# A two-block transformer kernel on one core: the first block's x turned and projected tile by tile, half of a modulation chunk computed later, x turned ahead of the weight splits, the last output tile in halves

## Chip, cores and metric

One core of a Trainium2 chip runs the whole program. The metric is the device time of one execution in microseconds (us), lower is better. The profile names the engines PE (TensorE), PEld (its weight loads), DVE (VectorE), ACT (ScalarE), POOL (GpSimd) and SP (SyncE, which here only issues transfers).

## What is computed

256 tokens with 1024 features go through two blocks of two layers each, all in float32. The first block, for each layer `l`:

```
h = x @ w_in[l]                      # 1024 x 5024: latents, two gates, q, k, v, 2048 merge gates
# latent attention (8 heads) from rms-normed latents, differential attention (4 heads)
merged = sigmoid(gates)[:, :1024] * (y_a @ w_branch_a[l]) + sigmoid(gates)[:, 1024:] * (y_b @ w_branch_b[l])
x = layer_norm(DEEPNORM_ALPHA * x + merged @ w_out[l])
```

The second block modulates with vectors made from a condition `c`, and a second stream `ctx` has its own condition:

```
mod_lat = silu(c) @ mod_w[i] + mod_b[i]          # 9 vectors of 1024 a layer, 1024 x 9216 weights
mod_ctx = silu(c_ctx) @ mod_w[0] + mod_b[0]
x = half_ffn(x); ctx = half_ffn(ctx)             # h = x * (1 + scale) + shift; swiglu, 1024 -> 2816 -> 1024
x = window attention over x and ctx (layer 0) or Fourier mixing (layer 1); x = half_ffn(x)
```

The output is x, 256 x 1024 float32.

## The kernel before

**Products in three parts.** A float32 product is made of three matmuls in a rounded format (`product`, L598 to L600): high part of x by high part of w, high x by low w, low x by high w. Weights come in 1 MB transfers into five slots of `raw`, two "pieces" of 128 x 1024 in each. For every piece ACT writes the high part (`w_hi`, L1173, six places), then DVE the low part (`w_lo`, L1545, ten places). `split()` on either engine is one piece. PE takes a piece with `piece()` and frees it with `piece_done`; 490 pieces go through in all. A piece of 512 columns is 12 matmuls.

**x turned.** Before a projection PE transposes x (two tiles, `t`, of 128 tokens) into PSUM banks `turn0`, `turn1`, `score0`, `score1`; ACT writes `xT_hi`, DVE `xT_lo`. In the first block and ahead of the first FFN, `turn` goes over both tiles and `project` starts once both are there. Elsewhere in the second block `turn_tile` and `project_first` (PE) with `second_tile` (ACT, DVE) turn and project tile 0 while tile 1 is still being normed. `keep_busy` issues matmuls whose result nobody reads.

**Modulation vectors.** DVE multiplies `mod_w` rows by silu(c), feature group by feature group (`mod_feature`, L1666: once into `acc_ctx` for the ctx condition, once into `mod_run` for c). POOL loads the weights, two feature groups to a 512 KB transfer (L492), into a ring of two places: a transfer is issued when DVE has used up the one two before. Eight groups, f0 to f7, make a chunk of 512 columns; then PE sums it over partitions with 16 small matmuls (`mod_sum`, L727), and DVE stores the result (`mod_store`). Each layer of the first block does six chunks, five of them for both conditions; the fifth of these (chunk 4) is done during the last projection and the layer norm. On POOL the first chunk of a layer waits for x of both tiles, and between its fourth transfer and the next chunk's first stand `b_merge` (two of 1 MB) and the `ln_rows` (two of 512 KB).

**Order.** All engines run lists written out by hand, with semaphores; what stands ahead on an engine's list delays what stands behind. `layer_norm` on DVE (L1635 to L1646) and `norm_root` on ACT (L1237, L1239) share the norm, tile after tile.

## Time and profile before

| | |
|---|---|
| time, median of 3 runs | 1633.92 us (1633.36 to 1637.47) |
| the profiled execution: its time, its span | 1632.27 us, 1630.5 us |
| PE busy | 1568.3 us, 96% of the span |
| DVE, ACT, POOL busy | 1204.2, 795.6, 156.2 us |
| transfers | 349.61 MB, 214 GB/s on average |
| granted PE clock, mean | 0.989 |

Busy time of PE is the sum over its matmuls as far as they don't overlap, those of `keep_busy` among them; its idle time is the rest, 62 us. A row of the timeline gives start, length, engine, line, operation, tensors, shape, how many instructions are merged in it, and in brackets how long the engine sat idle before it and what ended that.

### The profile page before, as it was taken

The page shows a single profiled execution, that of the slowest core. Times are in us where ns is not written, and L with a number is a line of the kernel's source. Part 1 is how long each engine was busy: PE and PEld are TensorE (multiplying, and loading weights), DVE is VectorE, ACT ScalarE, POOL GpSimd, SP SyncE. Part 2 cuts the span into 40 slices and gives each one's busy share as a digit, 9 for nine tenths or more (in the row PEclk, how much of TensorE's full clock was granted, in tenths as well). Part 3 has the DMA queues.
Part 4 walks back from the last instruction along what each step waited for, and adds up shares of the span by engine and source line. Part 5 has one row for each costly group of instructions (what it writes and reads, how often), then busy time and mean ns, then how long its engine had stood idle before and what let it go on. Part 6 is the DMA issues. An engine that isn't in the chain of part 4 may idle for free.

```text
span 1630.5 us, 20592 instructions
## 1 busy us (share of the span) xinstructions
PE 1568.3 (96%) x7685; PEld 1297.5 (80%) x7685; DVE 1204.2 (74%) x1852; ACT 795.6 (49%) x1243; POOL 156.2 (10%) x212
## 2 busy tenths in 40 slices
PE   6999989999999999999999899999999999999997
PEld 6888868888778887788877558888888888788886
DVE  6888888888877775777858867877587775575554
...
GB/s 282 306 225 166 157 158 301 245 184 142 172 220 264 285 271 234 194 277 277 271 167 196 123 1 232 281 277 278 209 235 279 282 274 181 91 210 190 181 182 77
DMA packets 200508, 349.61 MB, mean 214 GB/s; under 512 B 11189, under 2 KB 128237, under 8 KB 199901
## 3 DMA queue, kind: packets, MB, share of 16 engines
...
HBM read 347.21 MB, written 1.08 MB: 214 GB/s over the span
## 4 chain that ended last, share of the span: by engine, by line
PE 85%; DVE 10%; ACT 1%; DMA 1%; issue 1%; SPq 0%; DVEq 0%; POOLq 0%; ACTq 0%
PE acc L598 25%; PE acc L600 25%; PE acc L599 25%; DVE w_lo L1545 2%; PE turn L962 1%; PE acc L868 1%; PE score L848 1%; PE score L1058 1%; DVE acc_ctx L1666 1%; DVE x L1646 1%; DVE att_work L2126 1%; PE turn L857 1%; DMA raw<-in_w_in 1%; DMA mod_raw<-in_mod_w 1%; DVE wide L1879 1%
## 5 line engine op out<-in xcount | busy, mean ns | idle before, releaser
L1545 DVE TENSOR_TENSOR w_lo<-raw,w_hi 128x1024 fp32r<-128x1024 f32 (+2 forms) x490 | 584.3, 1200 | 258.5 <-ACT w_hi L1173 257.7
L1173 ACT ACTIVATE w_hi<-raw 128x1024 fp32r<-128x1024 f32 (+2 forms) x490 | 503.1, 1039 | 475.5 <-PE acc L600 439.3
L598 PE MATMUL acc<-w_hi,xT_hi 128*128 128x512 f32 (+1 forms) x1440 | 572.2, 397 | 10.2 <-issue 4.8
L600 PE MATMUL acc<-w_hi,xT_lo 128*128 128x512 f32 (+1 forms) x1440 | 562.1, 390 | 0.0
L599 PE MATMUL acc<-w_lo,xT_hi 128*128 128x512 f32 (+1 forms) x1440 | 561.4, 390 | 0.0
L598 PEld LDWEIGHTS acc<-w_hi,xT_hi 128*128 128x128 f32 x1440 | 271.8, 189 | 65.1 <-issue 12.0
L600 PEld LDWEIGHTS acc<-w_hi,xT_lo 128*128 128x128 f32 x1440 | 271.6, 189 | 57.0
L599 PEld LDWEIGHTS acc<-w_lo,xT_hi 128*128 128x128 f32 x1440 | 272.1, 189 | 52.8
L492 POOL DMA_DIRECT2D mod_raw<-in_mod_w x144 | 104.1, 723 | 924.0 <-DVE mod_run L1666 741.6
L598 PE MATMUL acc<-w_hi,hT_hi 128*128 128x512 f32 x440 | 172.8, 393 | 0.0
L600 PE MATMUL acc<-w_hi,hT_lo 128*128 128x512 f32 x440 | 171.4, 390 | 0.0
L599 PE MATMUL acc<-w_lo,hT_hi 128*128 128x512 f32 x440 | 171.3, 389 | 0.0
L1666 DVE SCALAR_TENSOR_TENSOR mod_run<-mod_raw,silu_c,mod_run 128x512 f32<-128x512 f32 x216 | 160.9, 745 | 5.1 <-DMA mod_raw<-in_mod_w 5.0
L598 PEld LDWEIGHTS acc<-w_hi,hT_hi 128*128 128x128 f32 x440 | 82.6, 188 | 18.3 <-issue 1.7
L600 PEld LDWEIGHTS acc<-w_hi,hT_lo 128*128 128x128 f32 x440 | 82.6, 188 | 17.4
L599 PEld LDWEIGHTS acc<-w_lo,hT_hi 128*128 128x128 f32 x440 | 82.7, 188 | 16.8
L1404 ACT ACTIVATE silu_g<-acc 128x256 f32<-128x256 f32 x110 | 36.3, 382 | 83.0 <-PE acc L600 83.0
L1237 ACT ACTIVATE turned<-x,neg_mean 128x1024 bf16<-128x1024 f32 x16 | 18.5, 1156 | 84.3 <-DVE neg_mean L1635 84.3
L1666 DVE SCALAR_TENSOR_TENSOR acc_ctx<-mod_raw,silu_c,acc_ctx 128x512 f32<-128x512 f32 x70 | 52.1, 744 | 6.0 <-DMA mod_raw<-in_mod_w 6.0
L2027 DVE TENSOR_TENSOR hidden<-acc,silu_g 128x256 f32<-128x256 f32 x110 | 41.5, 419 | 11.9 <-ACT silu_g L1404 8.2
L1313 ACT ACTIVATE work<-score,neg_max 128x256 f32<-128x256 f32 x64 | 29.6, 472 | 31.3 <-DVE neg_max L1785 31.3
L2034 DVE TENSOR_TENSOR hT_lo<-turn,hT_hi 128x512 fp32r<-128x512 f32 x55 | 38.0, 691 | 5.7 <-ACT hT_hi L1408 5.1
...
## 6 DMA issues: line engine op xcount, KB each, us to landing
...
```

The source lines that it names most:

```text
L492: pool.dma_start(mod_raw[:, s, :, :], w_mod[l, :, 2 * i:2 * i + 2, at]).then_inc(mod_in[s], 16)
L598: nc.tensor.matmul(dst, xh, wh, start=start, stop=False)
L599: nc.tensor.matmul(dst, xh, wl, start=False, stop=False)
L600: return nc.tensor.matmul(dst, xl, wh, start=False, stop=stop)
L1173: nc.scalar.activation(piece_part(w_hi[:, i % SPLIT_SLOTS, :], i), piece_part(raw[:, s, i % 2 * PIECE:(i % 2 + 1) * PIECE], i), ACT.Copy). ...
L1237: step(nc.scalar.activation(squares[:, t, :], x[:, t, :], ACT.Square, bias=neg_mean[:, t:t + 1], accum_out=square_sum[:, t:t + 1]))
L1313: m = nc.scalar.activation(p[:, t * TOK:t * TOK + TOK], bank[b][:, t * TOK:t * TOK + TOK], ACT.Exp, bias=neg_max[:, h, 2 * m_ + t:2 * m_ + ...
L1404: nc.scalar.activation(silu_g[:, half, t, :], bank[ACC[2 * half + t]][:, FC:2 * FC], ACT.Silu).then_inc(silu_done, 1)
L1545: nc.vector.tensor_tensor(piece_part(w_lo[:, i % RAW_PIECES, :], i), piece_part(raw[:, i // 2 % RAW_SLOTS, i % 2 * PIECE:(i % 2 + 1) * PIE ...
L1666: m = nc.vector.scalar_tensor_tensor(out=end if k == KD - 1 else run, in0=w, scalar=by, in1=run, op0=ALU.mult, op1=ALU.add)
L2027: nc.vector.tensor_tensor(hidden[:, half, t, :], bank[b][:, 0:FC], silu_g[:, half, t, :], ALU.mult).then_inc(moved[b], 1)
L2034: nc.vector.tensor_tensor(sl(hT_lo), bank[b][:], sl(hT_hi).bitcast(F32), ALU.subtract).then_inc(moved[b], 1)
```

## The change

1. *Start.* ACT no longer makes silu(c) and the exponential of lambda (each with a table load) ahead of the first splits; it does two splits instead of five before it writes `xT_hi`, and DVE likewise two instead of three. PE does 2 `keep_busy` matmuls instead of 6 and 5.
2. *Arrival of weights.* Each half of a slot has a semaphore of its own, and ACT's split of a piece waits for its half alone (except where halves are columns: the FFN's up weights).
3. *Tile by tile.* Layer 1's first projection and the first FFN's go through `project_first`. At the end of layer 0 the engines turn tile 0 with `plain_tile(0)` during tile 1's norm, at the end of layer 1 with `turn_tile`, as the second block does.
4. *Half of a chunk put off.* f4 to f7 of chunk 4 (and its `mod_sum`, now after the second projection) move from the end of a layer into the next layer's first splits, or the first FFN's (`owed`).
5. *Branches.* Feature groups of chunk 3 move: f3, f4 ahead of the second half of x, f5 alone between the branches, f6 and f7 in place of a split and f7. f0 to f2 of chunk 5 move from the small splits into the head transposes (`u` 3, 5, 7).
6. *Banks.* Transposes of heads begin with `score0` instead of `turn0`; PE's wait for all four banks before the scores is gone in the first block and is for `turn0` alone in the window attention. `q_a` and `k_a` are copied out half by half, and one split of a head stage moves behind the first head's exponentials.
7. *End.* The last tile's final operation and its output transfer are made in two halves of 512 columns.

```diff
-BRANCH_FEATURES = [(3, 4), (5, 6), (7,), ()]
+BRANCH_FEATURES = [(), (5,)]
+CHUNK_LATER = 4
-FIRST_SPLITS, HEAD_MORE = 1, (1, 4, 5)
+FIRST_SPLITS, HEAD_MORE = 1, (0, 1, 4, 5)
...
# SP
-                for rows in (slice(0, half), slice(half, 2 * half)):
-                    sp.dma_start(dst[:, rows, :], src[:, rows, :]).then_inc(raw_in[s], 16)
+                for i, rows in enumerate((slice(0, half), slice(half, 2 * half))):
+                    sp.dma_start(dst[:, rows, :], src[:, rows, :]).then_inc(raw_in[2 * s + i], 16)
-            for t in range(NT):
-                sp.wait_ge(x_ready, NT * 4 * LAYERS + t + 1)
+            for i, (t, at) in enumerate(((0, slice(0, D)), (1, slice(0, D // 2)), (1, slice(D // 2, D)))):
+                sp.wait_ge(x_ready, NT * 4 * LAYERS + i + 1)
...
# PE, at the head of each layer of the first block
-                after = turn(lambda t, k: x[:, t, k * P:k * P + P], x_tile, wait=(0, 6))
-                keep_busy("acc0", 5)
-                project(ACC[0:2], 4, n=LOW, after=after)
+                if l == 0:
+                    after = turn_x()
+                    keep_busy("acc0", 2)
+                    project(ACC[0:2], 4, n=LOW, after=after)
+                else:
+                    project_first(ACC[0:2], n=LOW)
                 project(ACC[2:4], 4)
+                if l:
+                    mod_sum(True)
...
-                        b = turn_bank((first + u) % 4)
+                        b = turn_bank((first + u + 2) % 4)
-                landed(*TURN, *SCORE)
...
                 project_by_tile(ACC[2:4])
-                mod_sum(True)
...
-            after = turn_x(wait=(0, 6))
-            keep_busy("acc0", 5)
-            after = ffn(after, True, turn_ctx_in, by_tile=False)
+            after = ffn(None, True, turn_ctx_in, by_tile=False, owed=True)
...
# ACT
-                    if i % 2 == 0:
-                        act.wait_ge(raw_in[s], 32 * c.next(f"raw{s}"))
+                    if not by_columns(i):
+                        act.wait_ge(raw_in[2 * s + i % 2], 16 * c.next(f"raw{2 * s + i % 2}"))
...
-            split(LEAD)
+            split(EARLY)
             for l in range(LAYERS):
-                turn_plain(xT_hi)
+                if l == 0:
+                    turn_plain(xT_hi)
+                    split(LEAD - EARLY)
+                    nc.scalar.activation(silu_c[:], cols[:, 0:2 * KD], ACT.Silu).then_inc(silu_ready, 1)
+                else:
+                    plain_tile(1)
...
-                norm_root()
+                norm_root(then=lambda: turn_tile(mod_lat[:, 0, :], 0, 0) if l else plain_tile(0))
...
# DVE
-                split_and_mod(8, range(8), True)
+                if l == 0:
+                    split_and_mod(8, range(8), True)
+                else:
+                    split_and_mod(4, range(CHUNK_LATER, KD), True)
+                    split_and_mod(4, range(0, 7), True)
...
                 m.then_inc(low_ready, 1)
+                if l:
+                    mod_store(*chunk_at(l - 1, 4))
+                    mods_stored()
+                    mod_feature(7, True)
...
-                split_and_mod(3, BRANCH_FEATURES[3], True)
-                split_and_mod(2, range(0, 4), True)
-                split_and_mod(1, range(4, 7), True)
+                split(4)
+                split_and_mod(2, range(CHUNK_LATER), True)
+                split()
...
-                mod_feature(7, True)
-                layer_norm(update, lambda t: wide[:, t, 0:D], between=split, at_root=lambda: mod_store(*ctx_chunk(4)))
-                mods_stored()
+                if l:
+                    layer_norm(update, lambda t: wide[:, t, 0:D], **by_tile)
+                else:
+                    layer_norm(update, lambda t: wide[:, t, 0:D], between=split, at_root=lambda: plain_tile(0))
```

**ACT at the program's start.** `modb` and `cols` are small inputs; `w_hi` rows are splits. Before, from the copy of `cols` to the first write of `xT_hi`:

```order
L1220 ACTIVATE cols<-turn 128x24 [waits turn1_full]
L1221 ACT_TABLE_LOAD
L1221 ACTIVATE silu_c<-cols 128x16 [waits act_step]
L1223 ACT_TABLE_LOAD
L1223 ACTIVATE lam_sum<-lam_sum 128x4 [waits lam_ready]
L1173 ACTIVATE w_hi<-raw 128x2x416 [waits piece_done,raw_in0]
L1173 ACTIVATE w_hi<-raw 128x2x416 [waits piece_done]
L1173 ACTIVATE w_hi<-raw 128x2x416 [waits piece_done,raw_in1]
L1173 ACTIVATE w_hi<-raw 128x2x416 [waits piece_done]
L1173 ACTIVATE w_hi<-raw 128x1024 [waits piece_done,raw_in2]
L1201 ACTIVATE xT_hi<-turn 128x512 [waits turn0_full]
```

And now:

```order
L1240 ACTIVATE cols<-turn 128x24 [waits turn1_full]
L1193 ACTIVATE w_hi<-raw 128x2x416 [waits piece_done,raw_in0]
L1193 ACTIVATE w_hi<-raw 128x2x416 [waits piece_done,raw_in1]
L1221 ACTIVATE xT_hi<-turn 128x512 [waits turn0_full]
L1221 ACTIVATE xT_hi<-turn 128x512 [waits turn1_full]
L1221 ACTIVATE xT_hi<-score 128x512 [waits score0_full]
L1221 ACTIVATE xT_hi<-score 128x512 [waits score1_full]
L1193 ACTIVATE w_hi<-raw 128x2x416 [waits piece_done,raw_in2]
L1193 ACTIVATE w_hi<-raw 128x2x416 [waits piece_done,raw_in3]
L1193 ACTIVATE w_hi<-raw 128x1024 [waits piece_done,raw_in4]
L1288 ACT_TABLE_LOAD
L1288 ACTIVATE silu_c<-cols 128x16
```

The four writes of `xT_hi` stand behind two splits instead of five, and behind no table load.

**DVE at the end of layer 0.** From tile 1's mean to the first operations on the turned x (`x_sum` belongs to the mean, `wide` holds the normed tile). Before:

```order
L1635 SCALAR_TENSOR_TENSOR neg_mean<-x_sum,mean_factor 128x1 [waits acc3_moved]
L1640 SCALAR_TENSOR_TENSOR wide<-x,neg_mean,ln_rows 128x1024 [waits mean_ready]
L1683 TENSOR_TENSOR mod_ctx<-score,modb 128x4 [waits score1_full]
L1684 TENSOR_TENSOR mod_lat<-score,modb 128x4
L1645 RECIPROCAL inv_std<-inv_std 128x1 [waits std_ready]
L1646 SCALAR_TENSOR_TENSOR x<-wide,inv_std,ln_rows 128x1024 [waits dve_step]
L1687 MEMSET free 128x1
L1581 SCALAR_TENSOR_TENSOR xT_lo<-turn,xT_hi 128x512 [waits turn_hi] x2
```

And now:

```order
L1663 SCALAR_TENSOR_TENSOR neg_mean<-x_sum,mean_factor 128x1 [waits acc3_moved]
L1668 SCALAR_TENSOR_TENSOR wide<-x,neg_mean,ln_rows 128x1024 [waits mean_ready]
L1760 SCALAR_TENSOR_TENSOR xT_lo<-turn,xT_hi 128x4x128 [waits turn_hi] x2
L1673 RECIPROCAL inv_std<-inv_std 128x1 [waits std_ready]
L1677 SCALAR_TENSOR_TENSOR x<-wide,inv_std,ln_rows 128x1024 [waits dve_step]
L1577 TENSOR_TENSOR w_lo<-raw,w_hi 128x2x416 [waits hi_ready]
L1760 SCALAR_TENSOR_TENSOR xT_lo<-score,xT_hi 128x4x128 [waits turn_hi] x2
```

Tile 0's `xT_lo` (128 x 4 x 128) stands inside tile 1's norm, ahead of tile 1's x.

**DVE in layer 1's first splits.** From the first split behind `gains` on. Before, where `TENSOR_SCALAR` is f0 of chunk 0:

```order
L1545 TENSOR_TENSOR w_lo<-raw,w_hi 128x1024 [waits hi_ready]
L1664 TENSOR_SCALAR acc_ctx<-mod_raw,silu_c 128x512 [waits ctx_step,mod_in0]
L1664 TENSOR_SCALAR mod_run<-mod_raw,silu_c 128x512 [waits mod_step]
L1545 TENSOR_TENSOR w_lo<-raw,w_hi 128x1024 [waits hi_ready]
L1666 SCALAR_TENSOR_TENSOR acc_ctx<-mod_raw,silu_c,acc_ctx 128x512 [waits ctx_step]
L1666 SCALAR_TENSOR_TENSOR mod_run<-mod_raw,silu_c,mod_run 128x512 [waits mod_step]
L1545 TENSOR_TENSOR w_lo<-raw,w_hi 128x1024 [waits hi_ready]
L1666 SCALAR_TENSOR_TENSOR acc_ctx<-mod_raw,silu_c,acc_ctx 128x512 [waits ctx_step,mod_in1]
L1666 SCALAR_TENSOR_TENSOR mod_run<-mod_raw,silu_c,mod_run 128x512 [waits mod_step]
```

And now:

```order
L1577 TENSOR_TENSOR w_lo<-raw,w_hi 128x1024 [waits hi_ready]
L1697 SCALAR_TENSOR_TENSOR acc_ctx<-mod_raw,silu_c,acc_ctx 128x512 [waits ctx_step,mod_in0]
L1697 SCALAR_TENSOR_TENSOR mod_run<-mod_raw,silu_c,mod_run 128x512 [waits mod_step]
L1577 TENSOR_TENSOR w_lo<-raw,w_hi 128x1024 [waits hi_ready]
L1697 SCALAR_TENSOR_TENSOR acc_ctx<-mod_raw,silu_c,acc_ctx 128x512 [waits ctx_step]
L1697 SCALAR_TENSOR_TENSOR mod_run<-mod_raw,silu_c,mod_run 128x512 [waits mod_step]
L1577 TENSOR_TENSOR w_lo<-raw,w_hi 128x1024 [waits hi_ready]
L1697 SCALAR_TENSOR_TENSOR acc_ctx<-mod_raw,silu_c,acc_ctx 128x512 [waits ctx_step,mod_in1]
L1697 SCALAR_TENSOR_TENSOR mod_run<-mod_raw,silu_c,mod_run 128x512 [waits mod_step]
L1577 TENSOR_TENSOR w_lo<-raw,w_hi 128x1024 [waits hi_ready]
L1697 SCALAR_TENSOR_TENSOR acc_ctx<-mod_raw,silu_c,acc_ctx 128x512 [waits ctx_step]
L1697 SCALAR_TENSOR_TENSOR mod_sum_lat<-mod_raw,silu_c,mod_run 128x512 [waits mod_step]
```

Four splits with f4 to f7 of chunk 4 come first; f0 of chunk 0 follows the fifth.

## Rows read from the trace of the kernel before

**Rows 1.** The page: busy time, share of the span, instructions.

```profile
PE 1568.3 (96%) x7685; PEld 1297.5 (80%) x7685; DVE 1204.2 (74%) x1852; ACT 795.6 (49%) x1243; POOL 156.2 (10%) x212
```

**Rows 2.** Who PE waited for: us in total, times, longest.

```profile
PE score L619 <- DVE mod_lat L1684: 5.0, 2, 2.6
```

**Rows 3.** Transfers by line: count, KB each, median us to landing.

```profile
raw<-in_w_in SPq DMA_DIRECT2D x8, 416.0 KB, 4.5
```

**Rows 4.** Timeline of the start.

```profile
5.03 26.66 SPq L394 DMA_DIRECT2D raw<-in_w_in  x14
...
12.39 1.06 PE L619 MATMUL score<-ident,x 128*128 128x128 f32 x4
...
18.88 1.06 ACT L1173 ACTIVATE w_hi<-raw 128x1024 fp32r<-128x1024 f32 x1 [2.35 <-DMA raw<-in_w_in]
...
21.40 0.43 PE L598 MATMUL acc<-w_hi,xT_hi 128*128 128x416 f32 x1 [3.09 <-DVE xT_lo L1581]
```

**Rows 5.** Timeline of the branches of layer 0.

```profile
187.37 0.43 DVE L1592 CAST xT_hi<-turned 128x512 fp32r<-128x512 f32 x1 [4.37 <-ACT turned L1210]
...
200.61 1.06 ACT L1173 ACTIVATE w_hi<-raw 128x1024 fp32r<-128x1024 f32 x1 [1.72 <-PE acc L600]
...
201.75 1.27 DVE L1879 SCALAR_TENSOR_TENSOR wide<-wide,acc 128x512 f32<-128x512 f32 x2
```

**Rows 6.** Timeline of PE in the first matmuls behind the branches.

```profile
211.72 0.63 PE L598 MATMUL acc<-w_hi,xT_hi 128*128 128x512 f32 x1
212.15 0.63 PE L599 MATMUL acc<-w_lo,xT_hi 128*128 128x512 f32 x1
...
214.62 0.39 PE L599 MATMUL acc<-w_lo,xT_hi 128*128 128x512 f32 x1
214.84 0.39 PE L600 MATMUL acc<-w_hi,xT_lo 128*128 128x512 f32 x1
```

**Rows 7.** Timeline of layer 0's end, up to ACT's copy of layer 1's first projection.

```profile
229.19 0.75 DVE L1666 SCALAR_TENSOR_TENSOR acc_ctx<-mod_raw,silu_c,acc_ctx 128x512 f32<-128x512 f32 x1 [2.36 <-DMA mod_raw<-in_mod_w]
229.85 0.74 DVE L1666 SCALAR_TENSOR_TENSOR mod_run<-mod_raw,silu_c,mod_run 128x512 f32<-128x512 f32 x1
...
235.94 0.99 PE L727 MATMUL score<-ones,mod_sum_lat 128*128 128x48 f32 x8
...
256.66 0.93 ACT L1260 ACTIVATE low<-acc 128x416 f32<-128x416 f32 x2 [1.14 <-PE acc L600]
```

**Rows 8.** Timeline of layer 1's end, up to the first FFN's first silu.

```profile
461.50 0.99 PE L727 MATMUL score<-ones,mod_sum_lat 128*128 128x48 f32 x8
...
485.64 0.66 ACT L1404 ACTIVATE silu_g<-acc 128x256 f32<-128x256 f32 x2 [1.60 <-PE acc L600]
```

**Rows 9.** Timeline of the window attention's end, up to its FFN's first silu.

```profile
995.14 0.61 PE L719 MATMUL score<-ones,ident 128*128 128x128 f32 x4
...
1012.03 0.66 ACT L1404 ACTIVATE silu_g<-acc 128x256 f32<-128x256 f32 x2 [0.24 <-PE acc L600]
```

**Rows 10.** Timeline of modulation loads and splits early in layer 1.

```profile
261.14 0.72 POOL L492 DMA_DIRECT2D mod_raw<-in_mod_w  x1 [4.20 <-DVE mod_run L1666]
...
279.30 0.49 DVE L1664 TENSOR_SCALAR acc_ctx<-mod_raw,silu_c 128x512 f32<-128x512 f32 x1 [4.05 <-DMA mod_raw<-in_mod_w]
...
280.11 1.22 DVE L1545 TENSOR_TENSOR w_lo<-raw,w_hi 128x1024 fp32r<-128x1024 f32 x1
```

**Rows 11.** The chain that ended last, in order of time: start, us, what.

```profile
278.43 1.72 PE score L727 x16
```

**Rows 12.** Timeline of PE around `q_a`'s copies and at the window attention's scores.

```profile
94.97 0.36 PE L598 MATMUL acc<-w_hi,cT_hi 128*128 128x256 f32 x1 [1.01 <-ACT work L1286]
...
909.84 0.66 PE L1058 MATMUL score<-kT,qT 64*128 64x512 f32 x1 [1.04 <-ACT kT L1441]
```

**Rows 13.** Timeline of the program's end.

```profile
1621.73 6.13 SPq L476 DMA_DIRECT2D out<-x  x2
...
1626.20 1.28 DVE L1646 SCALAR_TENSOR_TENSOR x<-gated,inv_std,ln_rows 128x1024 f32<-128x1024 f32 x1
```

181 lines of the change are left out of this document (115 added, 66 removed).

## The prediction

> **What bounds the kernel now.** The busy times come first: PE works 1568.3 us of the span [rows 1], so a change can only gain in its 62 idle us, in the `keep_busy` and low-clock matmuls that hide more of the same, and at the very end. Then who PE waits for: between projections it is the norm's chain, and at the branches `mod_lat`, twice, 2.6 us at the longest [rows 2]. Last the timelines of the places that the diff touches. The reader is to see there how long it takes from one projection's last result to the next one's first, since a `keep_busy` matmul counts as busy there. A steady matmul of 512 columns follows the one before by 0.22 us [rows 6], 12 of them make a piece: about 2.7 us. DVE needs 1.22 us for the low part of a piece [rows 10] and 2 x 0.66 for a feature group of both conditions [rows 7], ACT 1.06 for the high part [rows 4], so in a steady stretch PE is the slowest and splits run ahead of it. Of each term I therefore ask whether it shortens a turn, or takes the lead of the splits away.
>
> All sums go against the profiled execution: 1632.27 us, 1630.5 of them span. The median of the runs is 1.65 above that, and I keep this offset.
>
> **Start.** Before, ACT makes five splits ahead of the first `xT_hi`. The fifth waits 2.35 us for its weights and starts at 18.88 [rows 4]; `xT_hi` and `xT_lo` follow, and the projection starts at 21.40. Now only two splits stand ahead. Their halves of 416 KB are issued from 5.03 on [rows 4] and land 4.5 us after their issue [rows 3], before ACT is free. The transposes of x begin near 10.3 and cost 1.06 us for four [rows 4], 16 of them 4.2 us, so they end near 14.6; one copy by ACT (1.1) and one low part by DVE (0.6) behind the first bank put the projection's start near 15.1 to 15.6. That is 6 us earlier. The bounds are -8 (no table load is left in the way at all) and -4 (copies of the last banks and the low clock of the first matmuls). I take -6.0.
>
> At the cold start a transpose takes 0.265 us [rows 4], and behind the branches matmuls of one kind start 0.43 us apart first and 0.22 later [rows 6]: the lower granted clock, 1.2 GHz, and the higher. The idle PE at the branches precedes the slow ones. The Trainium skill, "TensorE: Matmul & The Clock Gate", section "What's actually happening", says that the throttled state is the default and activity releases it; that speaks against this term and for the turns: with 2 `keep_busy` matmuls in place of 11, the first matmuls would run slow. By that rule alone the start would give back up to half of its gain; the trace agrees as far as rows 6 go.
>
> **Heads.** PE waits 1.01 us for the copies of `q_a` [rows 12]; halves let it begin after one. But f0 to f2 of chunk 5 now stand between DVE's copies of the turned heads, and one split comes later. Between 0 and -1 per layer; I take -0.5, for two layers -1.0. At the window attention's scores 1.04 us is waited for `kT` [rows 12], and the bank order touches it: 0 to -1.0, I take -0.4.
>
> **Branches.** f3 and f4 ahead of the second half of x fill DVE's 4.37 us of idle time there [rows 5], at no cost; if that idle time were gone they would cost 2.6. Behind the second branch DVE's gate product starts at 201.75, although ACT's next split, which waited for PE, started at 200.61 [rows 5]: DVE was still at a split and f7. Now 4 feature operations (2.64 us) replace a split and two of them (2.5), and both are begun earlier, so the product can start at about 200.6. That shortens the wait for the turned `wide`: -1.1 per layer. Once PE starts earlier the slow matmuls behind it [rows 6] may vanish: nine at 0.43 instead of 0.22 are 1.9 us per layer. I take -2.1 for both layers; the bounds are 0 and -6.
>
> **Layer 0 to layer 1.** Before, 20.7 us go by from the `mod_sum` behind layer 0's last projection to ACT's copy of layer 1's first (235.94 to 256.66) [rows 7]. The window attention's end is already done tile by tile: 995.14 to 1012.03, 16.9 us [rows 9], for a first piece group of 512 columns; `low` has 416, so its 48 matmuls take 2.0 us less. The plain turn has two ACT copies and two DVE operations a tile instead of a column's scale and shift each: 1.1 to 1.5 less. That makes about 13.8, a gain of 6.9. The 16 matmuls of `mod_sum` take 1.72 us [rows 11]. Until now they lie in the norm's shadow, and in the new order they stand on PE's path behind the second projection: +1.8. Together -5.0, between -2 and -8.
>
> **Layer 1 to the FFN.** The same with modulated x: 461.50 to 485.64 is 24.1 us [rows 8], against 16.9 [rows 9]: -7.2, and the owed `mod_sum` adds 1.8. Together -5.3, between -3 and -8.
>
> **The owed half chunk.** This is the term against. f4 to f7 of chunk 4 are 8 operations, 5.3 us of DVE, and now stand ahead of chunk 0 among layer 1's first splits. What they push later is POOL's list. The fourth transfer of chunk 0 goes out at 261.14, then come `b_merge` and the `ln_rows`, and the next chunk's first group is not there before 279.30, with DVE idle for 4.05 us; its next split starts at 280.11 [rows 10]. So 18.2 us pass from the one to the other, and all of them move with the first. PE reaches the piece of that split at about 256.66 + 10 x 2.7 + 1.7 = 285.7 (ten pieces and a `mod_sum`), 4.4 us after its end at 281.3. In the new order the fourth transfer moves about 12 us later, measured from the start of layer 1's projection (four owed groups, four splits and a `mod_store` stand before it), while PE moves only 3.2 later (1.5 by the turn, 1.8 by `mod_sum`). 12 - 3.2 - 4.4 gives a stall of 4.5 us, and 0.8 for the next `mod_sum`: +5.2. The bounds are 0 (the transfers of `b_merge` land sooner) and +8. It would show as PE waiting on DVE's `w_lo`, or on `mod_sum_lat` first. At the FFN nothing of the kind stands on POOL's list, and DVE has time: 0.
>
> **End.** The last norm's product ends at 1627.5, and what is left of the span, 3 us, is the transfer [rows 13]. The second half's transfer starts when the whole one did, but is half as large. Were the 3 us all bytes, 1.5 would be saved, were they all fixed, nothing; I take a low value, -0.3, since the end of the program lies in them too. The Trainium skill, "DMA: Bandwidth & Descriptors", section "Anatomy of one DMA — SWDGE (gpsimd) path", splits a transfer into about 2.0 us fixed and the bytes by 436 GB/s, which for half of 512 KB gives an estimate of 0.6 us. No row here separates the two parts.
>
> **Sum.** -6.0 - 1.0 - 0.4 - 2.1 - 5.0 - 5.3 + 5.2 - 0.3 = -14.9. The profiled execution would go from 1632.3 to 1617.4, the median to 1619.
>
> **The rivals.** *A: no stall in layer 1, and the clock stays high.* Then +5.2 falls away, and up to 3.8 at the branches comes on top: 1608 to 1614. For it speaks that DVE stood idle 4.05 us just there, so that some delay is swallowed; against it that this idle time itself came from the late transfer [rows 10]. *B: PE's clock falls after the start and turns, or the stall takes 8 us.* The start is worth 3 instead of 6, the turns 3 each instead of 5: 3 + 4.3 + 2.8 less, 1626 to 1629. Rows 6 speak for it, rows 9 (a tile-wise turn without such a loss) against. *C: no change.* It would need the turns' gain to be lost, for example if tile 0's chain isn't ahead of tile 1's because DVE runs both in a row; 1629 to 1639. *D: slower.* One mechanism: the 18.2 us block on POOL's list behind the owed groups [rows 10] does not only delay one split but empties all the slots of `raw` and the ring, so that DVE and SP stay behind for the rest of layer 1. My stall is 5.2; it decides from 25 us on, which is more than the whole 18.2 us block. 1640 and more.
>
> **How the numbers follow.** The forecast, 1614 to 1624, has 0.5; A 0.2; B 0.16; C 0.08; D 0.06. Added up, the lower bounds would give 1602 and the upper 1633, but they fall together rarely. The range of 1609 to 1627 keeps the forecast, most of A and the lower part of B, and leaves out 2 in 10. A measurement here tells 0.3%, 4.9 us, from no change. Below 1629, faster by more than that, lie the forecast, A and B: 0.86; C is no difference to be told: 0.08; D is slower: 0.06.
>
> **What would show it.** The projection of layer 0 starts at 15 to 16 with one or two slow matmuls. From the last projection of a layer to the copy of the next first piece group 14 us, at the FFN 17. Behind `mod_lat` at the branches about 1.5 us of waiting instead of 2.6. In layer 1 a wait of PE for DVE, some 28 us after its first copy, of about 5 us; if there is none, A is right. DVE's busy time stays at 1204, since nothing is computed less. Wrong would be the sum if DVE's list in layer 1 kept the splits more than 8 us behind, or if the clock between the turned tiles fell to 1.2 GHz and stayed there.

## The result and the profile after

The changed kernel takes 1608.2 us (median of 4 runs, 1606.06 to 1613.27), the kernel before 1635.01 (4 runs, 1633.36 to 1637.47): ratio 0.9839, 95% interval 0.9809 to 0.9869. It is faster by 1.6%; in the two profiled executions the span goes from 1630.5 to 1604.4 us, -26.1. I had forecast 1619 with a range from 1609 to 1627: the direction was right, the gain was 27 us where I had 15, just outside the range. The four runs alone span both sides of its end at 1609, so what went wrong is read from the terms, not from the total.

The page of the changed kernel: its span, the busy times and the granted clock in 40 slices (tenths):

```profile
span 1604.4 us, 20702 instructions
...
PE 1558.9 (97%) x7671; PEld 1287.3 (80%) x7671; DVE 1201.3 (75%) x1853; ACT 795.5 (50%) x1250; POOL 154.2 (10%) x212
...
PEclk9999999999999999999999999999999999999999
```

Of the 26.1 us, 9.4 are busy time of PE: fewer matmuls that nobody reads, and fewer real ones at the low clock. To see where all of it comes from, I take the moment at which PE ends a piece (490 of them in each trace), and subtract; "by pieces" below means this difference. It stays flat through nearly all of the program and steps in a few places:

| stretch (pieces) | predicted | measured |
|---|---|---|
| start, to piece 15 | -6.0 | -7.3 |
| heads, two layers (15 to 54, 77 to 116) | -1.0 | -0.3 |
| branches, layer 0 (54 to 63) and layer 1 (116 to 127) | -2.1 | -5.5 and -5.3 |
| turn to layer 1 (63 to 67) and its `mod_sum` | -5.0 | -6.9 + 1.8 |
| stall in layer 1 (75 to 77) | +5.2 | +7.5 |
| turn to the FFN (127 to 131) and its `mod_sum` | -5.3 | -7.2 + 1.7 |
| context and window attention (200 to 287) | -0.4 | -4.2 |
| rest and end | -0.3 | -0.3 |
| sum | -14.9 | -26.1 |

Two rows carry the error: the branches (8.7 us more) and the attention (3.8 more). The others lie within 2.3 us each.

**Start.** Timeline of the changed kernel's start, to be held against [rows 4]:

```profile
10.34 0.90 ACT L1193 ACTIVATE w_hi<-raw 128x832 fp32r<-128x832 f32 x1 [0.29 <-DMA raw<-in_w_in]
...
12.47 1.08 ACT L1221 ACTIVATE xT_hi<-turn 128x512 fp32r<-128x512 f32 x2 [0.17 <-PE turn L633]
...
12.66 0.63 PE L633 MATMUL score<-ident,x 128*128 128x128 f32 x4
...
14.22 0.43 PE L612 MATMUL acc<-w_hi,xT_hi 128*128 128x416 f32 x1 [0.49 <-DVE xT_lo L1613]
```

The projection starts at 14.22 instead of 21.40. The last transposes already take 0.63 us for four instead of 1.06: the clock is at its higher level before the first product, so the slow matmuls that I had reckoned with don't come. That isn't so in every execution. The kernel that sums one projection later (below) has the same start, and its timeline is:

```profile
12.85 1.06 PE L633 MATMUL score<-ident,x 128*128 128x128 f32 x4
...
14.42 0.69 PE L612 MATMUL acc<-w_hi,xT_hi 128*128 128x416 f32 x1
14.91 0.55 PE L613 MATMUL acc<-w_lo,xT_hi 128*128 128x416 f32 x1
```

There the last transposes and the first matmuls are slow, and the first piece ends 1.0 us later.

**Branches.** Timeline of the changed kernel where the merged rows are turned (answering to [rows 5] and [rows 6]):

```profile
190.49 1.28 DVE L1959 SCALAR_TENSOR_TENSOR wide<-wide,acc 128x512 f32<-128x512 f32 x2
190.55 1.06 ACT L1193 ACTIVATE w_hi<-raw 128x1024 fp32r<-128x1024 f32 x1 [1.66 <-PE acc L614]
...
195.73 1.03 PE L633 MATMUL turn<-ident,wide 128*128 128x128 f32 x8
197.13 0.66 PE L633 MATMUL score<-ident,wide 128*128 128x128 f32 x4 [0.36 <-DVE wide L1964]
198.45 0.66 PE L633 MATMUL score<-ident,wide 128*128 128x128 f32 x4 [0.67 <-DVE wide L1964]
```

A window of the same kernel, four microseconds of the first projection behind it:

```profile
200.00:204.00 4.00, 4.00 (x18) 3.11 (x17) 4.00 (x5) 2.02 (x3) 0.00 (x0) 1.00 0.26 105
```

The kernel before, timeline:

```profile
197.83 1.06 ACT L1173 ACTIVATE w_hi<-raw 128x1024 fp32r<-128x1024 f32 x1 [1.60 <-PE acc L600]
...
204.40 1.09 PE L619 MATMUL turn<-ident,wide 128*128 128x128 f32 x8 [1.17 <-DVE wide L1884]
```

And its window:

```profile
208.00:212.00 4.00, 3.61 (x12) 2.87 (x13) 3.75 (x7) 1.77 (x3) 0.18 (x1) 0.50 0.46 131
```

In a window row the engines' busy time is followed by the granted clock (1.00, and 0.50 in the kernel before), the transfers' share and GB/s. DVE's gate product now starts with the end of the piece that it reads (190.49; ACT's split behind the same piece at 190.55). In the kernel before that same piece ended at 197.8, as ACT's split at 197.83 shows, and DVE, busy without a gap, began the product at 201.75: 3.9 us late. Three feature groups used to stand ahead of it and no longer do, f3, f4 and f6, together 3.96 us. DVE's idle time ahead of the second half of x, 4.37 us before [rows 5], is 1.71 us now: f3 and f4 lie in it, as forecast. PE's waits go from 1.17 + 2.69 + 0.21 to 0 + 0.36 + 0.67, 3.0 us less, and the clock behind them stays high, the other 2.5 of the 5.5 us.

**Layer 1's stall.** Timeline of the changed kernel early in layer 1, with what PE and DVE wait for:

```profile
264.29 1.22 DVE L1577 TENSOR_TENSOR w_lo<-raw,w_hi 128x1024 fp32r<-128x1024 f32 x1
264.43 1.19 PE L741 MATMUL score<-ones,mod_sum_lat 128*128 128x48 f32 x8 [3.98 <-DVE mod_sum_lat L1697]
...
272.56 0.49 DVE L1695 TENSOR_SCALAR acc_ctx<-mod_raw,silu_c 128x512 f32<-128x512 f32 x1 [7.05 <-DMA mod_raw<-in_mod_w]
```

The windows:

```profile
256.00:264.00 8.00, 4.46 (x20) 3.37 (x18) 7.43 (x26) 3.43 (x5) 1.62 (x3) 1.00 0.97 374
264.00:272.00 8.00, 7.57 (x28) 6.51 (x29) 1.51 (x2) 2.48 (x4) 0.74 (x1) 0.58 1.03 393
```

PE stands 3.98 us at the sum of chunk 0, because DVE finished f7 only at 264.3, and then runs at about half the clock (0.58 in the window). Ahead of that f7 DVE itself waits for the loads of the features; what DVE waited for from 240 to 267 us:

```profile
DVE acc_ctx L1697 <- DMA mod_raw<-in_mod_w: 2.3, 3, 1.3
DVE acc_ctx L1695 <- DMA mod_raw<-in_mod_w: 1.6, 1, 1.6
```

That is 1.64, 0.56, 1.32 and 0.40 us, 3.92 in all, as long as PE's wait. The other variants with this turn and four owed groups agree within 0.15 us: 6.44 us of such waits and 6.52 at the sum (loads of the next chunk first), 3.54 and 3.62 (`b_merge` early), 4.61 and 4.60 (features back), 5.59 and 5.67 (ACT's old start), 3.43 and 3.40 (old banks), 3.37 and 3.51 (later start). So the stall is as long as DVE's waits for the two-place ring of loads; that it would go with them fits, but no run removes them. Behind f7 DVE waits 7.05 us for the next chunk's f0, with the transfer engines full (1.03, 393 GB/s) of weights, `b_merge` and `ln_rows`. The prediction had the place (4.05 us of DVE's idle time grew to 7.05, the first sign at `mod_sum_lat`), but neither the waits ahead of f7 nor the slow matmuls behind the stall.

**Turns.** The changed kernel from the end of layer 0 to the first copy of layer 1, against [rows 7]:

```profile
223.51 1.04 PE L651 MATMUL turn<-ident,x 128*128 128x128 f32 x8
...
229.07 1.04 PE L651 MATMUL score<-ident,x 128*128 128x128 f32 x8
...
236.87 0.92 ACT L1302 ACTIVATE low<-acc 128x416 f32<-128x416 f32 x2
```

From the last projection (223.2) it is 13.6 us to the copy; I had worked out 13.8. PE has no wait between 215 and 240 us. In the kernel before it had two, 1.36 us for tile 0's x and this one:

```profile
242.44 0.69 PE L619 MATMUL score<-ident,x 128*128 128x128 f32 x2 [2.37 <-DVE mod_lat L1684]
...
242.75 1.28 DVE L1646 SCALAR_TENSOR_TENSOR x<-wide,inv_std,ln_rows 128x1024 f32<-128x1024 f32 x1
...
245.35 0.60 PE L619 MATMUL turn<-ident,x 128*128 128x128 f32 x4
```

The wait is for the store of the sums, which stands in tile 1's norm and frees the bank. Behind it come the 12 listed matmuls that nobody reads, so that tile 1, ready at 244.0, is turned from 245.35 on: the prediction has `mod_sum` in the norm's shadow, and it was not wholly there. This is also where the 5.0 us of [rows 2] belong: 2.37 us in this turn and 2.6 in the one to the FFN. The prediction puts them at the branches; PE's waits there are for `wide`.

### The profile page after: what moved, and what is told of

Same layout as the page of the kernel before. It is cut to its first block, busy times and chain, and to the rows that moved or that the text cites. A ratio compares the mean times of both kernels' runs of the same rounds, so it can differ in the third digit from the quotient of the medians.

```text
span 1604.4 us, 20702 instructions
## 1 busy us (share of the span) xinstructions
PE 1558.9 (97%) x7671; PEld 1287.3 (80%) x7671; DVE 1201.3 (75%) x1853; ACT 795.5 (50%) x1250; POOL 154.2 (10%) x212
## 4 chain that ended last, share of the span: by engine, by line
PE 82%; DVE 11%; DMA 3%; issue 1%; ACT 1%; SPq 0%; DVEq 0%; POOLq 0%; ACTq 0%
PE acc L612 24%; PE acc L614 24%; PE acc L613 24%; DMA mod_raw<-in_mod_w 2%; DVE w_lo L1577 2%; PE turn L982 1%; PE acc L889 1%; DVE acc_ctx L1697 1%; PE score L869 1%; DVE att_work L2200 1%; PE score L1077 1%; PE score L741 1%; DVE mod_run L1697 1%; PE turn L878 1%; DVE x L1677 1%
## 5 line engine op out<-in xcount | busy, mean ns | idle before, releaser
L613 PEld LDWEIGHTS acc<-w_lo,hT_hi 128*128 128x128 f32 x440 | 82.7, 188 | 16.5
```

Source lines behind the costliest of these rows:

```text
L613: nc.tensor.matmul(dst, xh, wl, start=False, stop=False)
```

## The experiments

Each experiment is an edit of the kernel after, or of the kernel before, and was timed with runs of the kernel before between its own. The medians of "before" in the four sets were 1633.3, 1634.1, 1631.7 and 1631.8 us; the changed kernel itself stood in none of them, so I compare by the ratio to before (0.9839 for it) and by pieces in the profiles. Its own interval is 0.3% on either side, about 5 us, so between variants a ratio tells only more than that; what is smaller is read by pieces, from one execution each.

**Features back in their old places.**

```diff
-BRANCH_FEATURES = [(), (5,)]
+BRANCH_FEATURES = [(3, 4), (5, 6)]
-                for k in (3, 4):
-                    mod_feature(k, True)
-                for k in (6, 7):
-                    mod_feature(k, True)
+                split_and_mod(1, (7,), True)
-                split(4)
+                split(3)
```

> The changed kernel with the branch features where they were (f3, f4 and f5, f6 with the first branch's splits, f7 with a split behind the second branch's first half). Theory: with them DVE is 2.64 us (f3, f4) + 1.32 us (f6 ahead) late at the second branch's first gate product, so PE waits about 3 us more per layer, and its granted clock falls to 0.5 behind that wait, which costs about 2.6 us more: 5.5 per layer, +11 us in all (ratio to the changed kernel 1.007). Rival (the place of the features is worth the 1.1 us per layer of my sum, the rest of the measured 5.7 is a clock that happened to stay high): +2 to +5 us, and the clock behind the branches stays at 1.00.

1619.74 us, ratio 0.9917 (0.9895 to 0.9938): 11.5 us above the changed kernel by the medians, 13 by the ratios. By pieces, layer 0's branches lose 4.9 us and layer 1's 5.2. The waits of before come back to the hundredth, and so does the clock. The timeline:

```profile
196.70 1.09 PE L633 MATMUL turn<-ident,wide 128*128 128x128 f32 x8 [1.17 <-DVE wide L1962]
200.49 1.11 PE L633 MATMUL score<-ident,wide 128*128 128x128 f32 x4 [2.69 <-DVE wide L1962]
```

Its window behind them:

```profile
200.00:204.00 4.00, 3.30 (x11) 2.58 (x12) 3.75 (x7) 1.47 (x3) 0.48 (x1) 0.50 0.46 131
```

The theory holds, and the rival falls: it is this edit, not chance, that keeps the clock. The branches make 10 us of it; another 1.4 lie in the first FFN, whose code is the same.

**The same edit alone, in the kernel before.** The same three moves, made in the old code.

```diff
-BRANCH_FEATURES = [(3, 4), (5, 6), (7,), ()]
+BRANCH_FEATURES = [(), (5,), (7,), ()]
                 mod_store(*ctx_chunk(2))
+                for k in (3, 4):
+                    mod_feature(k, True)
...
-                split_and_mod(1, BRANCH_FEATURES[2], True)
+                for k in (6, 7):
+                    mod_feature(k, True)
...
-                split_and_mod(3, BRANCH_FEATURES[3], True)
+                split(4)
```

> The kernel before with only the branch features moved (f3, f4 into DVE's idle time ahead of the second half of x, f5 alone between the branches, f6 and f7 where a split and f7 stood). Theory: -11 us against the kernel before (1.635 ms to about 1.624 ms, ratio 0.993), the wait for the second half of the merged rows falls from 2.7 to about 0.4 us and the clock stays at 1.00. Rival (1.1 us per layer, the rest belongs to other parts or chance): -2 to -5 us.

1628.48 us, ratio 0.9974 (0.9955 to 0.9993): 4 to 5 us, not 11. That is the rival's number, but not for its reason. By pieces the branches do give 5.5 and 5.3 us, but 2.1 and 2.4 us are lost again at the two turns. The timeline of the first:

```profile
233.15 1.09 PE L727 MATMUL score<-ones,mod_sum_lat 128*128 128x48 f32 x8 [1.24 <-DVE mod_sum_lat L1666]
...
237.13 1.11 PE L619 MATMUL turn<-ident,x 128*128 128x128 f32 x4 [2.00 <-DVE x L1646]
```

PE now reaches the end of the layer before DVE has f7 of chunk 4. The kernel before has no such wait there [rows 7]. So it is probably the half chunk put off that lets the branches' gain through; in the sum it stood only as a cost. No run moves both in the kernel before, and the run with two owed groups below, where each end of a layer gets slower again, is the nearest evidence.

**Matmuls that nobody reads, at the branches of the kernel before.** Two doses.

```diff
+                keep_busy("acc0", 10)
                 after = turn(merged, group_ready=merged_half, groups=range(2))
+                keep_busy("acc0", 20)
                 after += turn(merged, lambda: pe.wait_ge(merged_ready, c.next("merged")), groups=range(2, 4))
```

> The kernel before with 10 and 20 matmuls that nobody reads ahead of the two transposes of the merged rows, so that PE isn't idle there; DVE's list is as before. It parts the two halves of the 5.5 us per layer. Theory: the waits' 3 us stay, the 2.6 us of low clock go: -5 us in all (ratio 0.997), granted clock 1.00 behind the branches. Rival (DVE's chain would set the end there anyway and swallows what the clock gives): 0 to -1 us although the clock is at 1.00.

1636.21 us, ratio 1.002 (1.0006 to 1.0034): no faster. The clock is at 1.00, but each call shows as two listed matmuls in the timeline:

```profile
206.07 4.63 PE L719 MATMUL acc<-ones,ident 128*128 128x128 f32 x40
210.54 1.04 PE L619 MATMUL score<-ident,wide 128*128 128x128 f32 x8
```

They end more than 2 us after the time at which the wait ended before (208.18), so the dose hides the answer. With 5 and 9 calls instead of 10 and 20:

> The kernel before with 10 and 18 listed matmuls that nobody reads at the branches instead of 20 and 40, which ended 2 us after the merged rows were there. Theory: the clock stays at 1.00 behind the branches and the wait itself stays: about -2.3 to -2.6 us a layer behind the branches. What comes out at the end may be less, since at the turn into the next layer PE then waits for mod_sum_lat (1.3 us in both earlier variants of before) and its clock there is 0.5 instead of 0.85: -2 us in all, or nothing. Rival: 5 us faster, the full sum.

1633.64 us, ratio 1.0003 (0.999 to 1.0016). By pieces the branches are 2.0 and 1.7 us shorter, with the clock at 1.00 and PE still waiting for the same rows of `wide`; the turns are 2.4 and 2.7 us longer, PE standing at `mod_sum_lat` (0.65 us) and then for x (1.99). So the low clock is worth about 2 us a layer and the waits the other 3, and in this kernel nothing of it arrives, because PE meets DVE's features at the end of the layer.

**`b_merge` and `ln_rows` behind the next chunk's loads.** In the changed kernel:

```diff
                 mod_load(0, bass.ds(l * (5 * 512), 512))
+                mod_load(0, bass.ds(l * (5 * 512) + 512, 512))
                 for t in range(NT):
                     pool.dma_start(wide[:, t, GATES:GATES + 2 * D], a["b_merge"][l].partition_broadcast(P)).then_inc(bias_in, 16)
                 norm_rows(a["ln_gamma"][l], a["ln_beta"][l])
-                mod_load(0, bass.ds(l * (5 * 512) + 512, 512))
```

> The changed kernel with b_merge and the ln_rows loaded behind the next chunk's four modulation loads instead of ahead of them, in both layers. Theory: the block of transfers between the first and the second chunk makes DVE wait 7 us for f0 in layer 1, and PE 3 to 4 us behind that; without it -4 us (-2 to -7.5), and of the 7.5 us that layer 1 loses between its third and fifth group of projections at most the wait for mod_sum_lat is left. Rival (DVE is late by the 5.3 us of owed feature operations themselves, the transfers are hidden): within 1 us of the changed kernel, same wait of 4 us at mod_sum_lat. A third: the later b_merge makes the heads' gate additions wait: slower by some us.

1607.19 us, ratio 0.9834 (0.9811 to 0.9857): no difference to the changed kernel that can be told, where -4 us was expected. DVE's 7 us wait is gone, but by pieces the stall is 3.0 us longer. In the timeline PE stands longer at the sum:

```profile
267.13 1.94 PE L741 MATMUL score<-ones,mod_sum_lat 128*128 128x48 f32 x8 [6.52 <-DVE mod_sum_lat L1697]
```

So these transfers don't set that wait, as the rival has it, but the wait doesn't stay at 4 us either. In this trace DVE waits 1.93, 1.82 and 2.69 us for the loads of chunks 4 and 0 themselves, 6.44 in all.

**Two owed groups instead of four.**

```diff
-CHUNK_LATER = 4
+CHUNK_LATER = 6
...
-                        if features:
+                        if i < len(features):
                             mod_feature(features[i], ctx_too, into)
```

> The changed kernel with only f6 and f7 of chunk 4 put off instead of f4 to f7. In layer 1 PE now stands 3.98 us for mod_sum_lat (chunk 0's f7 comes too late: two owed transfers of 512 KB and four of its own, each issued when its place in the ring is free) and then runs some 12 matmuls at 0.50 of the clock, 7.5 us in all. Theory: one transfer less ahead of it is worth about 5 us, so that wait and the slow matmuls go, -5 to -7.5 us there; at each layer's end two more feature groups (1.3 us each) stand ahead of the norm and may give back up to 2.6 us. In all -2 to -6 us. Rival (the late loads don't matter, only that mod_sum stands ahead of the projections): no change in layer 1, slower by up to 5 at the layers' ends.

1607.09 us, ratio 0.9835 (0.9819 to 0.9852): no difference to the changed kernel that can be told. PE's wait at the sum falls from 3.98 to 1.35 us, and the clock stays high. By pieces layer 1's stall is 5.9 us shorter up to piece 77, of which the next two pieces give 1.9 back, and the ends of the layers with their turns cost 2.4 and 1.6 more. The stall is as expected, but the ends cost 4.0 us and not at most 2.6, so nothing is left of the 2 to 6 us: the half chunk's size trades one for the other.

**PE sums chunks 0 and 1 one projection later in layer 1.**

```diff
-                    if n % 2 == 0:
+                    if n % 2 == l:
                         mod_sum(True)
```

> The changed kernel where in layer 1 PE sums chunks 0 and 1 one projection later (behind the second and fourth of the four, not the first and third). DVE's work and all transfers keep their order. Theory: PE no longer stands 3.98 us for mod_sum_lat and its clock doesn't fall behind it: -5 to -7 us, if the splits of the projection that is now passed are there in time. Rival (DVE itself is late: its next split stands behind a wait of 7.05 us for the next chunk's f0, so PE stands there instead of at the sum): -1 to 0 us, the wait appears at w_lo. A third: DVE now waits for the later sum ahead of its store and falls behind: slower.

1610.42 us, ratio 0.9855 (0.9839 to 0.9872), and by pieces layer 1 is 2.5 us longer. The wait at the sum is gone, and in the timeline PE stands 7.8 us at splits instead:

```profile
265.80 0.50 PE L612 MATMUL acc<-w_hi,xT_hi 128*128 128x512 f32 x1 [1.92 <-DVE w_lo L1577]
274.70 0.79 PE L612 MATMUL acc<-w_hi,xT_hi 128*128 128x512 f32 x1 [5.88 <-DVE w_lo L1577]
```

That is the rival's mechanism, at a higher price than its 0: DVE's next splits stand behind the wait of 6.89 us for f0.

**`b_merge` early, alone and with the later sums.** POOL loads `b_merge` once tile 0 of x is normed (223 us), when the transfer engines are about to be idle.

```diff
-                pool.wait_ge(x_ready, c.next("x", 2))
+                pool.wait_ge(x_ready, c.next("x"))
+                for t in range(NT):
+                    pool.dma_start(wide[:, t, GATES:GATES + 2 * D], a["b_merge"][l].partition_broadcast(P)).then_inc(bias_in, 16)
+                pool.wait_ge(x_ready, c.next("x"))
                 mod_load(0, bass.ds(l * (5 * 512), 512))
```

> The changed kernel with each layer's b_merge (2 x 1 MB) loaded as soon as tile 0 of x is normed, while the transfer engines are almost idle (227 to 236 us), instead of between the first two chunks. Theory: two causes stand one behind the other in layer 1. The wait of 3.98 us at mod_sum_lat comes from the pace of the feature loads and stays, the 7.05 us for which DVE waits for the next f0 comes from b_merge and goes; PE hides the second behind the first now, so -0 to -2 us only. Rival (b_merge's bytes are what slows the feature loads too): -5 to -7 us.

1606.94 us, ratio 0.9838 (0.9814 to 0.9863), the same as the changed kernel, as the theory has it: DVE's wait falls from 7.05 to 1.01 us, PE's stays. The timeline:

```profile
264.89 1.46 PE L742 MATMUL score<-ones,mod_sum_lat 128*128 128x48 f32 x8 [3.62 <-DVE mod_sum_lat L1698]
...
266.99 0.48 DVE L1696 TENSOR_SCALAR acc_ctx<-mod_raw,silu_c 128x512 f32<-128x512 f32 x1 [1.01 <-DMA mod_raw<-in_mod_w]
```

> Both: b_merge loaded early, and PE's sums of chunks 0 and 1 one projection later in layer 1. Theory of the two causes: only with both gone the loss of layer 1 goes: -5 to -7.5 us against the changed kernel, about 1.601 ms. Rival (a third cause stands behind them, such as DVE waiting for the later sum or being late by the owed 5.3 us itself): -0 to -2 us, with a new wait at w_lo.

Both together: 1603.05 us (1600.98 to 1607.19), ratio 0.9827 (0.9798 to 0.9856), the lowest median of all. Against the changed kernel that is 5 us by the medians but only 2 by the ratios, with intervals that overlap: the time alone doesn't show the gain. By pieces layer 1 is 5.8 us shorter than in the changed kernel, with a single wait of 1.75 us left in the timeline:

```profile
265.21 0.50 PE L613 MATMUL acc<-w_hi,xT_hi 128*128 128x512 f32 x1 [1.75 <-DVE w_lo L1578]
```

The windows show the clock at 1.00 throughout:

```profile
256.00:264.00 8.00, 7.46 (x33) 5.83 (x32) 7.83 (x27) 3.79 (x5) 0.72 (x1) 1.00 1.00 369
264.00:272.00 8.00, 6.79 (x30) 5.63 (x31) 7.02 (x11) 5.09 (x7) 1.46 (x2) 1.00 0.91 311
```

By pieces, in layer 1 one edit alone gives 0.4 us, the other alone costs 2.5, and both together give 5.8: the two causes stood one behind the other. That the program gets faster by as much is not shown.

**Both tiles turned ahead of the first projection.** Layer 1 and the first FFN only.

```diff
                     keep_busy("score0", 8)
+                if whole:
+                    keep_busy("score0", 32)
+                    after.append(turn_tile(1))
                 for t in range(NT):
...
-                            if i == 2:
+                            if i == 2 and not whole:
```

> The changed kernel with PE turning both tiles before the first projection of layer 1 and of the first FFN (32 more matmuls that nobody reads in between), DVE and ACT as they are. Theory: what the tile-wise order gives in the two turns (measured 6.9 and 7.2 us between the last projection and the first copy) is mostly tile 0's matmuls lying in tile 1's norm: 24 matmuls of 416 columns (4.6 us) and 24 of 512 (5.5 us), so +9 to +11 us. Rival (the gain is the shorter chain of copies and the kept clock): +0 to +4 us.

1622.32 us, ratio 0.9925 (0.9908 to 0.9942): +14. But 80 listed matmuls keep PE from 224.57 to 233.5, while tile 1's x was there at 228.2, so this is their number and not the order. With 8 calls in place of the 32:

> As the run with both tiles turned ahead of the first projections of layer 1 and the first FFN, but with 16 listed matmuls in between that nobody reads instead of 64: in that run they kept PE until 233.5 us, although tile 1's x was ready at 228.2, so its +6.6 us at the turn is mostly their number. Theory now: what overlaps tile 1's norm are the 12 matmuls of tile 0 ahead of the second transposes (2.3 us), and another 12 lie in the copies; +2 to +3 us at the first turn, +2.5 to +3.5 at the second, +5 in all. Rival: as first expected, +9 to +11 us.

1612.48 us, ratio 0.9877 (0.985 to 0.9904). By pieces the turn to layer 1 is 1.5 us longer and the one to the FFN 4.2, 5.7 in all where 5 was expected, but split otherwise. The lap of tile 0's matmuls over tile 1's norm is worth at most that much of the 6.9 and 7.2, since 16 listed matmuls stand in it too. The rest of the turns' gain I did not take apart; what else changed there is where the copies stand on ACT's and DVE's lists, the matmuls that nobody reads, and the store of the sums that PE no longer waits for.

**ACT's start as before.**

```diff
+            act.wait_ge(moved[b], 2)
+            nc.scalar.activation(silu_c[:], cols[:, 0:2 * KD], ACT.Silu).then_inc(silu_ready, 1)
-            split(EARLY)
+            split(LEAD)
             for l in range(LAYERS):
                 if l == 0:
                     turn_plain(xT_hi)
-                    split(LEAD - EARLY)
-                    nc.scalar.activation(silu_c[:], cols[:, 0:2 * KD], ACT.Silu).then_inc(silu_ready, 1)
```

> The changed kernel with ACT's start as before: silu(c) with its table load and five splits ahead of the first xT_hi. Theory: this order makes up nearly all of the 7.2 us gained at the start, of which the fifth split waits for its weights until 18.9: first projection at 20 to 21 us instead of 14.2, +6 to +7 us. Rival (the arrival half by half and the missing matmuls that nobody reads give part of it): +3 to +4 us.

1613.31 us, ratio 0.9875 (0.9859 to 0.9892), and by pieces 5.2 us later at the end of the start: between the two. The timeline:

```profile
15.27 1.06 ACT L1193 ACTIVATE w_hi<-raw 128x1024 fp32r<-128x1024 f32 x1 [0.15 <-DMA raw<-in_w_in]
...
17.80 0.43 PE L612 MATMUL acc<-w_hi,xT_hi 128*128 128x416 f32 x1 [2.84 <-DVE xT_lo L1613]
```

The fifth split starts at 15.27 and not at 18.88 [rows 4]: lambda's exponential with its table load stayed away, and a split waits for its own half of a slot. So the order of ACT's list is worth 5.2 of the 7.3 us. These two, DVE's shorter list and PE's fewer matmuls that nobody reads share the rest; no run parts them.

**Old banks in the window attention, and a start that is only later.** The first edit:

```diff
-                    b = turn_bank((u + 2) % 4)
+                    b = turn_bank(u % 4)
...
-                landed(TURN[0])
+                landed(*TURN, *SCORE)
```

> The changed kernel with the old order of banks and the wait for all four of them in the window attention only. Theory: PE waits 1.04 us again for kT's last copy instead of 0.25, so the scores' stretch (71.05 us between two pieces around it, in other variants of the changed kernel 69.7 to 72.1) is 0.8 us longer, and all else of the 2.6 us is the place where the clock falls: +0.8 us, blurred by +-1.5. Rival (the banks give the 2.6 us): a stretch of 73.7 us as in the kernel before, +2.6 us.

1611.35 us, ratio 0.9871 (0.9854 to 0.9888): 3 us above the changed kernel by the medians, 5 by the ratios and by pieces. PE's wait for `kT` is 1.0 us again. The stretch around the scores takes 72.76 us; in the changed kernel 71.05, in its other variants 69.7 to 72.1, before 73.68. Taken alone this looks undecided. But the stretch hangs together with the projection ahead of it, which has two lengths, 14.9 and 16.5 us:

| kernels | projection | around the scores | both, from the gap of 2.40 us on |
|---|---|---|---|
| new banks, 5 variants | 16.5 | 69.7 | 116.6 |
| new banks, the changed kernel and 5 variants | 14.9 | 71.1 to 72.1 | 116.3 to 117.3 |
| old banks, this run | 16.5 | 72.8 | 119.6 |
| old banks, before and its variants (4) | 14.9 or 16.5 | 72.1 to 75.5 | 117.9 to 120.8 |

So this one edit costs 3.3 us against the changed kernel and 3.0 against the five with the same projection. In those five the clock stays at 1.00 through the scores, and here it falls; the windows of the run with two owed groups and of this one:

```profile
898.00:906.00 8.00, 7.56 (x58) 4.37 (x55) 5.91 (x17) 5.72 (x18) 3.18 (x4) 1.00 0.22 70
898.00:906.00 8.00, 6.79 (x38) 3.24 (x39) 4.77 (x17) 4.62 (x14) 1.09 (x2) 0.79 0.43 155
```

The expectation of 0.8 us is wrong, and its rival of 2.6 nearer. Another 1.4 us of this run's 5.2 lie in the first FFN, whose code is the same.

```diff
-                    keep_busy("acc0", 2)
+                    keep_busy("acc0", 10)
```

> The changed kernel with 16 listed matmuls more that nobody reads ahead of the first projection, nothing else. Theory: the start is 1 to 2 us later, and untouched stretches of the second block come out at one of two lengths that differ by 1.6 us (14.9 or 16.5 us for the projection ahead of the attention, 146.4 or 148.0 in the first FFN) as the clock falls in their 2.4 us gap or not, so that the total is +1 to +2 us, +-3. Rival (these lengths belong to the variants' edits, not to their timing): every untouched stretch as in the changed kernel, and exactly the start's delay in all.

1608.15 us, ratio 0.9854 (0.9837 to 0.9871). The first piece ends 1.30 us later, the last one 1.62; in between the difference runs through 0.92, 0.43, 1.38, 2.98 and back to 1.68. The step from 1.38 to 2.98 lies in the second block's projection ahead of the attention, whose code and data are the same in both kernels. The changed kernel's timeline there:

```profile
836.55 0.47 PE L612 MATMUL acc<-w_hi,xT_hi 128*128 128x512 f32 x1 [2.40 <-issue]
```

Its window:

```profile
838.00:842.00 4.00, 4.00 (x19) 3.30 (x18) 2.51 (x5) 3.39 (x5) 0.00 (x0) 1.00 0.23 87
```

The shifted kernel, timeline:

```profile
837.93 0.47 PE L612 MATMUL acc<-w_hi,xT_hi 128*128 128x512 f32 x1 [2.40 <-issue]
```

and window:

```profile
838.00:842.00 4.00, 4.00 (x12) 3.14 (x13) 3.00 (x7) 2.03 (x4) 0.00 (x0) 0.63 0.55 205
```

So the same idle time of 2.40 us is followed by a clock of 1.00 in the one and 0.63 in the other. Over all profiled kernels this stretch takes 14.9 us (8 of 16) or 16.5 (8 of 16), never between. What it loses here the scores give back: 1.3 us, the step from 2.98 to 1.68.

## Why the prediction was wrong

**Branches: the step that failed.** The prediction says that the gate product "can start at about 200.6", read off an ACT split that waited for PE, and -1.1 us per layer. That split belongs to a later piece. The product needs the piece that ends at 197.8, so DVE was 3.9 us late and not 1.1, and all of it was the features that the change moves. The other half of the step, the slow matmuls, stood in the bounds ("may vanish", 1.9 us a layer) but not in the sum; they vanished. Measured: -5.5 and -5.3 for -2.1 in all, shown by putting the features back (+4.9 and +5.2), with the waits at 3.0 us a layer and the clock at some 2. The sign that the prediction names, a shorter wait behind `mod_lat` at the branches, could not come: that wait is at the turns.

**Attention: mis-sized.** -4.2 for -0.4. The prediction priced the banks by the one wait that names `kT`, 1.04 us. Putting them back costs 3.3 us over the two stretches: PE waits 1.0 us for `kT` in place of 0.2 to 0.3, 1.6 us for `ctx_area` in place of 0.4 to 0.9, and the clock falls in the scores; for the last two the sum had no term. The two lengths of the projection ahead are not the change's, but they don't explain the row either: what the projection gains the scores lose, to within 1 us, in all eleven kernels with the new banks. What makes the rest of the 4.2 us, 0.9, is open. Why the clock falls behind one gap of 2.4 us and not behind another stays open too; a shift in time alone can decide it.

**The owed half chunk: the place right, the size and the price of the wait wrong.** I charged it with a stall of 5.2 us by a chain of POOL's transfers. The stall is 7.5: 4.0 of waiting at `mod_sum_lat`, the rest half-clocked matmuls. The chain in the prediction starts behind chunk 0's last load, with `b_merge`. That makes DVE wait, as I had it, but it is not what PE waits for first: moving it away changes nothing as long as the sum stands ahead. PE's wait comes from the loads before it, 3.92 us of DVE's waits at the ring of two. The working has small slips, none of which matters: ten pieces and a sum from 256.66 on end at 285.4, not 285.7, and 12 - 3.2 - 4.4 is 4.4. What I did not see is that without the half chunk the branches' gain would probably not have reached the end (11 us became 4 to 5 in the kernel before). A sum of terms can't show this: the terms are not independent.

**Start: -7.3 for -6.0, in part luck.** The mechanism was right. I started it near 15.1 at the earliest, it began at 14.22, and the low clock was over by then. The last transposes ran fast ahead of any idle matmul. In two variants with the same start (the later sums, and `b_merge` early) the first four matmuls ran slow and the first piece ended 1.0 and 1.2 us later. The kernel before has the same spread: its first piece ends at 23.9, in two of its variants with the same start at 25.4 and 26.3. So the 7.3 us hold for these two executions. The Trainium skill, "TensorE: Matmul & The Clock Gate", section "What's actually happening", has the throttled state as the default. The trace agrees: the first twelve transposes ran slow. It cost this term nothing here and about 1 us in those two variants, not half of the gain.

**Turns: right.** -5.1 and -5.5 for -5.0 and -5.3, worked out from the same kind of turn elsewhere in the trace [rows 9]. The reason given for `mod_sum` was not quite right: before, its store held PE up in the turn. **Heads:** -0.3 for -1.0; probably the features between the copies gave back what the halves won, which no run tests. **End:** -0.3, as said, and too small for a run to test by itself. The two traces do part the fixed share from the bytes; of the output transfers, before and after, us to landing:

```profile
out<-x SPq DMA_DIRECT2D x2, 512.0 KB, 2.6
out<-x SPq DMA_DIRECT2D x2, 256.0 KB, 2.0
```

Half the bytes save 0.6 us of the transfer, as the estimate beside this term has it, though that one is for transfers that GpSimd issues and SyncE issues these. At the program's end 0.4 us of it arrive.

Rival A had the time (1608 to 1614) but not the reason: it wanted no stall, and the stall came, larger than forecast. Of its two conditions the second, the clock at the branches, was true. Added up, the prediction's own lower bounds give about 1600 (it says 1602), so the measured time lay within them; the range ended at 1609 because they were not expected together. The branches alone passed their bound of -6 by 4.8 us and the attention its -1.0 by 3.2; without these two the time would lie inside.

## What to carry to other kernels

To find how late an engine is, take the instruction whose result it reads and that one's end, not the next release that happens to be near in time; here 1.1 us instead of 3.9. Where a helper engine carries work that may be done at any time, such work has to be followed to the place where it is due: moving it out of one wait gave 11 us at the branches, but by itself only 4 to 5 of them reached the end of the program. In the changed kernel, where another part moves its due date too, the same move is worth all of it. To size a stall of PE behind a helper, add up what the helper itself waited for ahead of the result that PE reads; here the two agree within 0.15 us. Two waits that stand one behind the other, each alone worth nothing, are found by removing both. And a stretch whose length varies is to be compared together with its neighbour, and among kernels whose neighbour has the same length.

## What the runs showed of the chip

A wait can cost PE more than its length. Behind 3.98 us of waiting the granted clock was 0.50 from 265.3 to 272.1 us. Around the 2.69 us at the branches it was 0.50 until 214.5 in the kernel before and until 205.4 in the run that restored its features, 6.3 and 4.9 us behind the wait's end. Behind 0.36 and 0.67, and behind 1.75 us in the run with both edits, it stayed at 1.00.

Behind a gap of 2.40 us in unchanged code it stayed at 1.00 in half of the profiles and fell in the others (0.63 in a window of one), worth 1.6 us each time, and 1.3 us of delay at the start were enough to change which. The same kernel's own runs differ by 7 us, and the mean granted clock goes with it: 0.995 in both of 1606.06 us, 0.993 at 1610.35, 0.992 at 1613.27. So such steps are a likely part of the spread; which stretches they lie in isn't known, since the profiles are of one execution each.
